# Sparse attention with the keys on partitions: maxima a head ahead, sums from a column of ones

## The reference

```python
s_c = einsum(q, k_cmp) * scale          # 31 compressed keys
p_c = masked_softmax(s_c, cmp_end <= t);  o_c = p_c @ v_cmp
s_s = einsum(q, k_selected) * scale     # 8 blocks of 64, all selected here
p_s = masked_softmax(s_s, key <= t);      o_s = p_s @ v_selected
s_w = einsum(q, k_window) * scale       # window of 512
p_w = masked_softmax(s_w, causal);        o_w = p_w @ v_window
o = g0 * o_c + g1 * o_s + g2 * o_w;       out = (o * silu(z)) @ w_out
```

## Time and profile before

| | us |
|---|---|
| median of 3 runs | 1100.11 |
| lowest, highest run | 1088.68, 1100.58 |
| span of the profiled execution | 1095.5 |
| TensorE busy (matmul) in the span | 1032.5 (94%) |
| TensorE weight loads | 890.5 (81%) |
| VectorE, ScalarE, GpSimd busy | 467.6, 445.3, 410.1 |

### The profile page before, as it was taken

One profiled execution on the slowest core, in us unless ns is written; L12 is line 12 of the kernel. 1 busy time (PEld: TensorE's weight loads), 2 busy tenths in 40 slices (PEclk: granted clock), 3 DMA queues, 4 the chain that ended last, 5 costly groups with the idle time before them and its releaser, 6 DMA issues. The chain is left out here.

```text
span 1095.5 us, 17295 instructions
## 1 busy us (share of the span) xinstructions
PE 1032.5 (94%) x6326; PEld 890.5 (81%) x6326; DVE 467.6 (43%) x1234; ACT 445.3 (41%) x1156; POOL 410.1 (37%) x560
## 2 busy tenths in 40 slices
PE   5999989999999998999999999999999989989798
PEld 5988878898898986888888778887888778878676
DVE  3231036666666654211110146675354465465421
ACT  4353346555555544313421223443344444444320
POOL 1453355545545443333533246585011111111131
PEclk8999999999999999999999999999678998999999
DMA  5322221010110102132632113222000000000021
GB/s 172 119 99 90 83 64 42 21 42 22 42 42 22 60 1 77 39 115 74 139 111 76 39 52 103 83 77 77 1 1 1 0 0 0 0 0 1 1 97 58
DMA packets 42444, 58.74 MB, mean 54 GB/s; under 512 B 8821, under 2 KB 25482, under 8 KB 42378
## 3 DMA queue, kind: packets, MB, share of 16 engines
q1 hardware_dynamic: 40672, 57.42, 17.0%
q10 hardware_dynamic: 1706, 0.43, 0.2%
HBM read 55.62 MB, written 2.10 MB: 53 GB/s over the span
## 5 line engine op out<-in xcount | busy, mean ns | idle before, releaser
L92 PE MATMUL bank<-w_hi,h_hi 128*128 128x512 f32 (+2 forms) x480 | 188.4, 393 | 6.7 <-DVE h_lo L1281 6.7
L94 PE MATMUL bank<-w_hi,h_lo 128*128 128x512 f32 (+2 forms) x480 | 184.3, 384 | 0.0
L93 PE MATMUL bank<-w_lo,h_hi 128*128 128x512 f32 (+2 forms) x480 | 184.3, 384 | 0.0
L1241 POOL TENSOR_TENSOR w_lo<-w_raw,w_hi 128x2048 fp32r<-128x2048 f32 (+1 forms) x26 | 118.6, 4562 | 174.2 <-ACT w_hi L1039 174.2
L1670 ACT ACTIVATE prob<-bank,negmax 128x128 f32<-128x128 f32 (+3 forms) x128 | 67.6, 528 | 145.9 <-DVE negmax L1736 145.7
L92 PEld LDWEIGHTS bank<-w_hi,h_hi 128*128 128x128 f32 x480 | 91.3, 190 | 25.9 <-DVE w_lo L1276 6.9
L1736 DVE TENSOR_REDUCE negmax<-bank 128x1 f32<-128x128 f32 (+3 forms) x128 | 62.0, 489 | 113.0 <-PE bank L1591 111.2
L1619 PE MATMUL bank<-kvr,probT 128*128 (+1 forms) x640 | 95.1, 282 | 12.8 <-ACT probT L1680 10.9
L1619 PEld LDWEIGHTS bank<-kvr,probT 128*128 128x128 f32 x640 | 88.6, 202 | 22.3 <-ACT probT L1680 19.6
L94 PEld LDWEIGHTS bank<-w_hi,h_lo 128*128 128x128 f32 x480 | 91.1, 190 | 17.1
L93 PEld LDWEIGHTS bank<-w_lo,h_hi 128*128 128x128 f32 x480 | 91.4, 190 | 15.7
(11 more groups left out here) (253 smaller groups left out, 2382.7 us busy)
## 6 DMA issues: line engine op xcount, KB each, us to landing
w_raw<-in_nsa_w_in SPq DMA_DIRECT2D x10, 1024.0 KB, 5.0
w_raw<-in_mla_w_in SPq DMA_DIRECT2D x8, 1024.0 KB, 5.1
w_raw<-in_mla_w_out SPq DMA_DIRECT2D x8, 1024.0 KB, 5.1
w_raw<-in_nsa_w_in SPq DMA_DIRECT2D x8, 984.0 KB, 5.0
w_raw<-in_mla_w_uq SPq DMA_DIRECT2D x16, 288.0 KB, 3.1
w_raw<-in_mla_w_ukv SPq DMA_DIRECT2D x16, 256.0 KB, 3.4
w_raw<-in_nsa_w_out SPq DMA_DIRECT2D x4, 1024.0 KB, 5.1
w_raw<-in_mla_w_in SPq DMA_DIRECT2D x4, 704.0 KB, 4.8
```

The source lines that it names most:

```text
L92: nc.tensor.matmul(out, a[0], b[0], start=start, stop=False)
L93: nc.tensor.matmul(out, a[0], b[1], start=False, stop=False)
L94: return nc.tensor.matmul(out, a[1], b[0], start=False, stop=stop)
L1241: nc.gpsimd.tensor_tensor(w_lo[g % 2][:, :, 0:width], w_raw[g % 2][:, :, 0:width], w_hi[g % 2][:, :, 0:width].bitcast(F32), ALU.subtract). ...
```

## The change

The scores of a head are made twice. `first_scores` makes one product only (high part by high part, plus the mask) with queries on partitions, for the next head, and VectorE takes the maxima from it. `turn_max` turns the 4 x 2 columns of negated maxima into rows, and ScalarE (`max_row`) writes them below the 96 rows of the queries' high part (rows 96 and 97); the keys' high part gets rows of ones (and a zero for the other branch), so that the product itself subtracts the maximum. The scores proper (`small_terms`, `large_term`) then have the keys on partitions: a block of 128 keys by all queries from its diagonal on. Their exponential, without bias or accumulator, is already what `values` needs as its stationary operand. The values get a 65th column of ones that gives the sums. A head has 6 units of scores in place of 8 on each side. The transposes of the probabilities, their copies and GpSimd's staged copy of the queries are gone; compressed scores take two products in place of three for each tile; every engine's program is written out for 16 heads, without a loop. The evacuation of the input projection's chunks 2 and 3 goes in three pieces for each tile in place of one.

In the diff the new stage stands without the removed lines (these are in the functions above), and its indentation is cut:

```diff
-KS, VS, KW, VW = 0, 384, 640, 1024
-KVR = 2 * CVW
+DV1 = DV + 1
+KS, VS, KW, VW = 0, G * DK, G * (DK + DV1), G * (2 * DK + DV1)
+KVR = 2 * G * (DK + DV1)
-kT_hi = at_slab("kT_hi", 104, [DK, 2, G, SEQ], F32R)
+kT_hi = at_slab("kT_hi", 104, [DK + 2, 2, G, SEQ], F32R)
-kcT_hi = at_slab("kcT_hi", 56.75, [DK, G, NC], F32R)
-kcT_lo = at_slab("kcT_lo", 57.25, [DK, G, NC], F32R)
+kcT = at_slab("kcT", 57, [DK, 2, G, NC], F32R)
...
-2: [(kvr, 2 * KV_W - CVW, 0, KV_W)], 3: [(kvr, 3 * KV_W - CVW, 0, KV_W)]}
+2: [flat(kvr, k0, 0, s_end), spaced(VS, s_end), flat(kvr, KW, w_start, KV_W)],
+3: [flat(kvr, KW + KV_W - w_start, 0, w_end), spaced(VW, w_end),
+    flat(kvr, KVR, w_end + G * DV, KV_W)]}
...
+for c0 in (VS, VW):
+    nc.gpsimd.memset(kvr[:, :, c0:c0 + G * DV1].rearrange("p t (g d) -> p t g d", g=G)[:, :, :, DV:DV1], 1.0)
...
+U = 6
+block_of = [(0, (0,)), (0, (1,)), (1, (0,)), (1, (1,)), (2, (0, 1)), (3, (0, 1))]
+tile_of = [(0, (0, 1)), (1, (0, 1)), (2, (0,)), (2, (1,)), (3, (0,)), (3, (1,))]
...
+probT = [at_slab(f"probT1_{a}", 10 * a, [P, cols]) for a in range(2)]
+qT_hi = [at_slab(f"qT_hi{a}", 20 + 2 * a, [DK + 2, SEQ], F32R) for a in range(2)]
+qT_lo = [at_slab(f"qT_lo{a}", 24 + 2 * a, [DK, SEQ], F32R) for a in range(2)]
...
+negmax = at_slab("negmax1", 58.5, [P, 2, NT, 2])
...
+first_bank, score_bank, x_bank = bank[0:2], bank[2:5], bank[7]
+o_most = bank[5][:, 0:3 * 2 * DV1].rearrange("p (i b d) -> p i b d", i=3, b=2)
+o_last = bank[6][:, 0:2 * DV1].rearrange("p (b d) -> p b d", b=2)
+cv_at = bank[6][:, 2 * DV1:2 * DV1 + NT * DV]
...
 @block.tensor
 def _(pe):
     def turn_q(n):
+        if n:
+            pe.wait_ge(m_in, n)
         for t in range(NT):
+            last = nc.tensor.transpose(x_bank[0:DK, t * P:(t + 1) * P],
+                                       qs[:, t, n * DK:(n + 1) * DK], ident[:, :])
+        last.then_inc(q_turned, 1)
+    def first_scores(n, u):
+        a, k = n % 2, U * n + u
+        i, branches = tile_of[u]
         tok, keys = slice(i * P, (i + 1) * P), (i + 1) * P
+        if u == 0:
+            pe.wait_ge(q_hi, n + 1)
+        if k >= 2:
+            pe.wait_ge(max_done, k - 1)
+        for w, b in enumerate(branches):
+            dst = first_bank[k % 2][:, w * keys:(w + 1) * keys]
+            nc.tensor.matmul(dst, qT_hi[a][0:DK, tok], kT_hi[0:DK, b, n // HPG, 0:keys],
+                             start=True, stop=False)
+            last = nc.tensor.matmul(dst[:, tok], identb[:, :], causal[:, :], start=False, stop=True)
+        last.then_inc(f_done, 1)
+    def turn_max(n):
+        pe.wait_ge(max_done, U * n + U)
+        if n:
+            pe.wait_ge(ct_ready, n)
+        else:
+            pe.wait_ge(q_lo, 1)
+        for i in range(NT):
+            last = nc.tensor.transpose(x_bank[0:2, i * P:(i + 1) * P], negmax[:, n % 2, i, :],
+                                       ident[:, :])
+        last.then_inc(m_turned, 1)
+    def small_terms(n, u, w, b):
+        a, g = n % 2, n // HPG
+        j, keys = block_of[u][0], slice(block_of[u][0] * P, (block_of[u][0] + 1) * P)
+        left = left_of(j)
+        dst = score_bank[(U * n + u) % 3][:, w * left:(w + 1) * left]
+        nc.tensor.matmul(dst, kT_hi[0:DK, b, g, keys], qT_lo[a][:, j * P:], start=True, stop=False)
+        nc.tensor.matmul(dst, kT_lo[:, b, g, keys], qT_hi[a][0:DK, j * P:], start=False, stop=False)
+    def large_term(n, u, w, b):
+        a, g = n % 2, n // HPG
+        j, keys = block_of[u][0], slice(block_of[u][0] * P, (block_of[u][0] + 1) * P)
+        left, rows = left_of(j), DK + 1 + b
+        dst = score_bank[(U * n + u) % 3][:, w * left:(w + 1) * left]
+        nc.tensor.matmul(dst, kT_hi[0:rows, b, g, keys], qT_hi[a][0:rows, j * P:], start=False, stop=False)
+        return nc.tensor.matmul(dst[:, 0:P], causal[:, :], identb[:, :], start=False, stop=True)
+    def scores(n, u):
+        k = U * n + u
+        if k >= 3:
+            pe.wait_ge(exp_done, k - 2)
+        for w, b in enumerate(block_of[u][1]):
+            small_terms(n, u, w, b)
+            last = large_term(n, u, w, b)
+        last.then_inc(s_done, 1)
+    def start_scores(n):
+        pe.wait_ge(q_lo, n + 1)
+        for u in range(2):
+            k = U * n + u
+            if k >= 3:
+                pe.wait_ge(exp_done, k - 2)
+            small_terms(n, u, 0, u)
+        pe.wait_ge(m_in, n + 1)
+        if n == 0:
+            pe.wait_ge(rows_set, 1)
+        for u in range(2):
+            large_term(n, u, 0, u).then_inc(s_done, 1)
+    def compressed_scores(n):
+        a = n % 2
+        pe.wait_ge(q_lo, min(n + 2, H))
         for i in range(NT):
             tok = slice(i * P, (i + 1) * P)
+            dst = x_bank[:, i * 2 * NC:(i + 1) * 2 * NC]
+            nc.tensor.matmul(dst, qT_hi[a][0:DK, tok], kcT[:, :, n // HPG, :], start=True, stop=False)
+            last = nc.tensor.matmul(dst[:, 0:NC], qT_lo[a][:, tok], kcT[:, 0, n // HPG, :],
+                                    start=False, stop=True)
         last.then_inc(c_done, 1)
+    def turn_compressed(n):
+        pe.wait_ge(c_exp, n + 1)
+        nc.tensor.transpose(x_bank[:, 0:P], c_e[:, :, :].rearrange("p i n -> p (i n)"),
+                            ident[:, :]).then_inc(ct_done, 1)
+    def compressed_values(n):
+        pe.wait_ge(ct_ready, n + 1)
+        nc.tensor.matmul(cv_at, c_eT[:, :], v_diag[:, n // HPG, :, :].rearrange("p i d -> p (i d)"),
+                         start=True, stop=True).then_inc(cv_done, 1)
+    def values(n, i):
+        pe.wait_ge(exp_done, U * n + (2, 4, 5, 6)[i])
+        if n and i == 0:
+            pe.wait_ge(o_left, 2 * n - 1)
+        if n and i == 3:
+            pe.wait_ge(o_left, 2 * n)
+            pe.wait_ge(cv_left, n)
+        for b in range(2):
+            c0 = (VS, VW)[b] + n // HPG * DV1
+            for j in range(i + 1):
+                at = at_of[j, b] + (i - j) * P
+                last = nc.tensor.matmul(o_most[:, i, b, :] if i < 3 else o_last[:, b, :],
+                                        probT[n % 2][:, at:at + P], kvr[:, j, c0:c0 + DV1],
+                                        start=j == 0, stop=j == i)
+        if i >= 2:
+            last.then_inc(pv_done, 1)
     turn_q(0)
+    for u in range(U):
+        first_scores(0, u)
+    turn_max(0)
+    for n in range(H):
+        more = n + 1 < H
+        start_scores(n)
+        if more:
+            turn_q(n + 1)
+        scores(n, 2)
+        scores(n, 3)
+        values(n, 0)
+        scores(n, 4)
+        if more:
+            first_scores(n + 1, 0)
+            first_scores(n + 1, 1)
+        scores(n, 5)
+        compressed_scores(n)
+        values(n, 1)
+        if more:
+            first_scores(n + 1, 2)
+            first_scores(n + 1, 3)
+        values(n, 2)
+        turn_compressed(n)
+        if more:
+            first_scores(n + 1, 4)
+            first_scores(n + 1, 5)
+        values(n, 3)
+        compressed_values(n)
+        if more:
+            turn_max(n + 1)
 @block.scalar
 def _(act):
+    def high(n):
+        act.wait_ge(q_turned, n + 1)
+        nc.scalar.activation(qT_hi[n % 2][0:DK, :], x_bank[0:DK, :], ACT.Copy).then_inc(q_hi, 1)
+    def exponential(n, u):
+        k = U * n + u
+        j, branches = block_of[u]
+        wide = len(branches) * left_of(j)
+        at = at_of[j, branches[0]]
+        act.wait_ge(s_done, k + 1)
+        nc.scalar.activation(probT[n % 2][:, at:at + wide], score_bank[k % 3][:, 0:wide],
+                             ACT.Exp).then_inc(exp_done, 1)
+    def max_row(n):
+        act.wait_ge(m_turned, n + 1)
+        nc.scalar.activation(qT_hi[n % 2][DK:DK + 2, :], x_bank[0:2, :], ACT.Copy).then_inc(m_in, 1)
+    high(0)
+    max_row(0)
+    for n in range(H):
+        exponential(n, 0)
+        exponential(n, 1)
+        if n + 1 < H:
+            high(n + 1)
+        for u in range(2, U):
+            exponential(n, u)
+        act.wait_ge(c_shift, n + 1)
+        nc.scalar.activation(c_e[:, :, :], c_s[:, :, :], ACT.Exp).then_inc(c_exp, 1)
+        if n + 1 < H:
+            max_row(n + 1)
 @block.gpsimd
 def _(pool):
     o = Order(pool, pool_s)
+    o.link(nc.gpsimd.memset(kT_hi[DK:DK + 2, :, :, :].bitcast(F32), 1.0))
+    nc.gpsimd.memset(kT_hi[DK:DK + 1, 1, :, :].bitcast(F32), 0.0).then_inc(rows_set, 1)
+    for n in range(H):
+        pool.wait_ge(o_left, 2 * n + 2)
+        pool.wait_ge(cv_left, n + 1)
         o.link(nc.gpsimd.tensor_tensor(o_c[:, :, :], o_c[:, :, :], o_sw[:, :, 0, :], ALU.add))
         o.link(nc.gpsimd.tensor_tensor(o_c[:, :, :], o_c[:, :, :], o_sw[:, :, 1, :], ALU.add))
+        at = z_sb[:, :, n * DV:(n + 1) * DV]
         nc.gpsimd.tensor_tensor(at, o_c[:, :, :], at, ALU.mult).then_inc(mixed, 1)
 @block.vector
 def _(dve):
     o = Order(dve, dve_s)
+    def low(n):
+        dve.wait_ge(q_hi, n + 1)
+        nc.vector.tensor_tensor(qT_lo[n % 2][:, :], x_bank[0:DK, :], qT_hi[n % 2][0:DK, :].bitcast(F32),
+                                ALU.subtract).then_inc(q_lo, 1)
```

(68 more changed lines are left out.)

273 lines of the change are left out of this document (40 added, 233 removed).

## The result

The changed kernel takes **1055.61 us** in the median of 4 runs (1054.56 to 1056.62) where the kernel before took 1098.40 beside it: ratio 0.9625, 95% interval 0.9587 to 0.9662. In a second series it was 1056.63, ratio 0.9626 (0.9575 to 0.9678). The profiled execution took 1056.62 with a span of 1054.8. Where the runs of one kernel differ by more than a per cent, the clock granted over the whole execution differs with them.

A forecast was written before the change was run, and what follows sets the result against it. TensorE, busy nearly throughout, loses time to waits and a low clock; its work does not shrink. Stage 247.6 against 272.5 us, 24.9 less: 1100.1 - 24.9 + 1.5 = 1077 us, range 1063 to 1107.

The forecast's parts named there:

- A: Rival, the forecast itself: after head 0 the clock holds but for +1.5 us, giving 1077 us; chance 0.45.
- S: Start of a head's first small term on TensorE, zero point of the walk; for head 0 at 7.35 us.
- The walk through a head: One head timed from its first small term through TensorE and VectorE to the next: 14.6 us a head.
- TensorE's work: TensorE's own work a head, summed part by part: 13.7 before, 13.8 us after, so not less.
- the 13.7: TensorE's own work a head in the kernel before: 15.41 us less 1.7 of waiting.
- What binds is VectorE's written order: VectorE's chain sets the head: last maximum at 14.0 us, TensorE ready at 13.2, one wait of 0.8.
- C: Rival: VectorE's chain ends before TensorE, a head is TensorE's 13.9 us, another 10 less, 1066; chance 0.09.
- Head 0 at the low clock: First 13 us of head 0 left at 1.2 GHz, as before: +5.9 us.
- Cheap gate product: VectorE's gate product costs 0.20, not 0.40, since GpSimd's three operations are over by 3 us into the head.
- What I costed at nothing: Loop's end, two waits more for each queue, 32 more short ScalarE copies: nothing, 2 us together if dear.
- B: Rival: the clock falls as often as before, costing 15 us, so 1090; chance 0.33.
- D: Rival: slower, the wait before `turn_max` and the start's idle 5 us keep the clock low, 1124; chance 0.13.

The follow-up runs named there:

- e10: e9 with 20 needless transposes a head that nobody waits for (output leaves the turning out): 1056.75 us, 0.9619 of the kernel before.
- e1: Changed kernel with tiles 0 to 2 scaled after the last two maxima, off VectorE's chain: 1058.42 us, 0.9644 of the kernel before.
- e8: e1 with both branches of tiles 0 and 1's first scores in one product and one mask: 1053.52 us, 0.9612 of the kernel before.
- e4: Changed kernel with three needless 512-column reductions in VectorE's chain of each head: 1100.35 us median (1082.09 to 1105.92), no ratio.
- e9: Kernel before without probability transposes, their copies and waits; values take unturned probabilities (output leaves the turning out): 1174.51 us, 1.0698.
- e11: e9 with 20 needless ordinary fp32r products of 128 columns a head (output leaves the turning out): 1227.59 us, 1.1174 of the kernel before.
- e14: Changed kernel with its 9 transposes a head as ordinary products (output leaves out the true queries): 1072.70 us, 0.9776 of the kernel before.
- e16: e9 with 8 needless ordinary 512-column products a head (output leaves the turning out): 1060.26 us, 0.9651 of the kernel before.
- e5: Kernel before with its hardware loop over pairs of heads written out, nothing else: 1094.85 us against 1097.51, 0.9970.
- e6: Kernel before with its 20 probability blocks a head turned by ordinary fp32r products with an identity, not transposes: 1238.96 us, 1.1212.
- e15: e9 with 4 needless transposes a head (output leaves the turning out): 1111.68 and 1185.06 us in its two runs, no ratio.

## Why the prediction was wrong, step by step

My stage had 249.1 us with A's 1.5 of low clock; it took 229.06. The 20.0 divide so:

| Term | predicted | measured | difference |
|---|---|---|---|
| start to S of head 0 (774.09 - 767.05) | 7.35 | 7.04 | 0.3 |
| head 0 (790.41 - 774.09) | 14.6 + 5.9 | 16.32 | 4.2 |
| heads 1 to 14 (981.51 - 790.41) | 14 x 14.6 | 191.1 = 14 x 13.65 | 13.3 |
| head 15 to GpSimd's end | 15.3 | 14.6 | 0.7 |
| low clock later | 1.5 | 0 | 1.5 |

Two of the predicted numbers hold slips of adding. The walk through a head ends at 14.05 + 0.44 = 14.5, and I went on with 14.6: 1.5 us in 15 heads. The terms of the start add to 6.6, or 7.2 with the row of maxima, and not to 7.35.

- **TensorE's work: right in the sum, in part by luck.** 13.8 forecast, 13.65 measured with no gap. `turn_max` took 0.36 of my bound of 0.44, the first scores 2.26 of 2.3 (those of tiles 0 and 1 0.87 of 0.9), compressed scores 0.89 of 0.9. But the value products cost 0.224 each (four from 838.74 to 839.64, eight from 842.40 to 844.19) where I had 0.205 and had named over 0.21 as a sign of being wrong: 0.4 us a head more. A part of it was offset by the 13.7 from which I counted, as e10's 13.49 for the old work outside the loop shows. "TensorE does not get less work" holds.
- **The step that failed: "What binds is VectorE's written order", the last maximum at S+14.0.** It ends at S+13.2 (843.28 + 1.28 - 831.38), TensorE is at `turn_max` at S+13.3, and the forecast wait of 0.8 is not there: TensorE's own work binds (e1, e8). The 0.8 divides so. VectorE began at S+7.55 (838.93 - 831.38), not S+7.7: 0.15. Its chain is 5.63 us (838.93 to 843.28 + 1.28); my terms for it add to 6.06, and gaps and rounding made 6.3 of them: 0.24. The terms themselves were 0.43 too long. I summed durations, and the rows show independent instructions of VectorE overlapping: two maxima of 384 are 1.01 long and the next instruction starts 0.93 after them (I had 1.1); the copy is 0.28 long, with 0.20 to the next start (I had 0.28); leaving three tiles took 0.90 (0.95), the last two maxima 1.28 (1.38), the compressed maximum 1.39 (1.43). I had named the sign (under 6 us speaks for C) and gave C 0.09 although a chain shorter by 0.7 us was enough for it.
- **The clock: right in direction, for a reason that is only half of it.** A said that it holds because waits go; it held wholly, from 781 to 988 us. e4 supports the wait's part: with two waits of 0.9 put back, three runs of four lost clock and one did not. The Trainium skill (TensorE: Matmul & The Clock Gate, "A second HAM failure mode: psum-queue depth-cycling") says that short idle gaps between groups of matmuls can drop the clock again and again; the 0.89 in e4's profile, with two waits of 0.9 a head, agrees. My other support, the rule of the Trainium skill that transposes don't count as busy ("PE-mode transpose" on the same page), is contradicted for the fp32 transposes of this kernel: 20 of them put back raised the clock from 0.50 to 1.00 (e9, e10), 20 ordinary products of the same columns did not (e11). The change took 20 of the things out that held the old clock up. What holds the new one is not shown: by e14 its 9 transposes are not needed once the clock is up, and for its wide products there is only e16.
- **Head 0 at the low clock: too dear.** I carried over 13 us from before; by the rows of 772 to 781 it was back at 1.00 at about 780, so some 6 us of head 0 were low. At my own 0.45 that is 2.7 on 13.65, and 16.32 was measured.
- **Cheap gate product: right** (0.17 long and 0.20 to the next start; my 0.20). GpSimd's three operations run from 832.46 to 834.82, long before it (841.98), so no contention is seen. The row of maxima has its cover, as forecast: 0.18 us a head, hidden.
- **What I costed at nothing:** the stage begins 0.4 later than before; the loop's end (e5) gave 2.7 us by the medians, with an interval that holds nothing. Behind the stage, 2.3 us that I had not thought of: the clock is 0.64 from 996 to 1004 us, where VectorE and ScalarE prepare and TensorE waits; in the first 8 us behind the old stage it was 0.80.
- **Rivals.** The outcome is A's clock with C's head. I had treated the two as separate cases with a low price each; in the changed kernel they go together, since a head in which VectorE is early is one without waits. (That a head without waits holds its clock is not so in e9 and e11.) Without A's 1.5 the pair gives 1100.1 - 24.9 - 15 x 0.7 = 1064.7 by my terms, inside my range. The profiled execution's 1056.6 lies 8.1 below: 3.5 of head 0, 3.5 of the 14 heads' last 0.25 us each, 1.0 of start and end, 2.8 less around the span (1.8 against 4.6), and 2.7 lost outside the stage. The 4.6 was wrong for the old kernel as well: it set one execution's span against the median of others, and in every run on record that has both, time and span differ by 1.8 to 2.0 us.
- **B and D** did not come, but both can: e4, with waits like those that they name, gave the gain back in three runs of four, and e6, e9 and e11 are slower than D by a clock that no wait brought down.

## What to carry to other kernels

Where an engine's chain and TensorE's work come out within a few per cent of each other, don't forecast the sum of durations: take distances between starts from the trace, for the order in which the instructions will stand. And ask of the case without waits which clock it would have, in place of pricing the two apart: here they went together in the changed kernel, and did not in e9 and e11. Look at the granted clock per stretch before counting instructions: at 0.50 with TensorE busy throughout, removing work (e9) made this kernel 7% slower, and adding useless transposes to that (e10) made it 10% faster.

## What the runs showed of the hardware

- TensorE can stay at 1.2 GHz for 406 us while the profile shows it busy in all of them (e6, 0.50 from 774 to 1180 us). It can also fall so: e11 was at 1.00 from 778 to 788 us and at 0.50 from 788 to 1000, busy throughout. The ends of its instructions are modelled, so gaps of a tenth of a us can be hidden in this.
- What TensorE executes changed its clock where no wait was added or taken away. From 786 to 1000 us it was 0.50 with nothing added (e9), 0.50 with 20 ordinary products of 128 columns a head (e11), 1.00 with 20 transposes (e10) and 0.97 with 8 ordinary products of 512 columns (e16). Why is open.
- The level can change several times in one stage: in e15 the clock was 1.00 at 820 to 840 us, 0.50 at 860 to 880, 1.00 at 900 to 920, and 0.50 from 940 us to the stage's end.
- Independent instructions of VectorE in a row overlap by some 0.08 us in the profile: a copy that is 0.28 us long (from 843.08) is followed at 843.28.
